# Entry of a two-block kernel: first modulation in column quarters, packed vectors on ScalarE's queue, angles ahead of the input, a late store of the input

## The reference

```
mod = silu(c) @ w_ada + b_ada            # 6 x 1024 columns: shift1, scale1, gate1, ...
u   = rmsnorm(x, g_mix) * (1 + scale1) + shift1
proj = u @ w_in                          # q, k, v, us (256 columns), two gates
y_ssm = s5(us; a_re, a_im, log_dt, b, c) # needs exp(log_dt), cos and sin of angles a_im*dt*2^j
```

## Time and profile before

| what | us |
|---|---|
| median of three runs (2013.05 to 2013.33) | 2013.3 |
| the profiled execution, its time | 2013.66 |
| the profiled execution, its span | 2011.9 |

### The profile page before, as it was taken

One profiled execution on the slowest core, in us unless ns is written; L12 is line 12 of the kernel. 1 busy time (PEld: TensorE's weight loads), 2 busy tenths in 40 slices (PEclk: granted clock), 3 DMA queues, 4 the chain that ended last, 5 costly groups with the idle time before them and its releaser, 6 DMA issues. The chain is left out here.

```text
span 2011.9 us, 25774 instructions
## 1 busy us (share of the span) xinstructions
PE 1980.5 (98%) x10047; PEld 1641.4 (82%) x10047; DVE 1100.9 (55%) x1349; ACT 647.8 (32%) x1068; POOL 1302.6 (65%) x757
## 2 busy tenths in 40 slices
PE   7999999999999999999999999999999999999998
PEld 4788988888788877888888888888888888888888
DVE  5981366767662686656622376722564554525554
ACT  4202333233431454444300045433434433211103
POOL 2638546656364459999845546876787888858650
PEclk9999999999999999999999999999999999999999
DMA  9535555544535213243573331343324222198332
GB/s 371 152 97 166 189 162 179 158 155 140 204 130 205 84 63 105 84 147 105 208 283 140 104 134 38 109 147 105 104 85 147 105 105 105 32 375 307 123 136 84
DMA packets 191945, 295.38 MB, mean 147 GB/s; under 512 B 15480, under 2 KB 139344, under 8 KB 191824
## 3 DMA queue, kind: packets, MB, share of 16 engines
q1 hardware_dynamic: 181840, 270.66, 39.6%
q10 hardware_dynamic: 9984, 23.07, 3.0%
HBM read 213.73 MB, written 79.97 MB: 146 GB/s over the span
## 5 line engine op out<-in xcount | busy, mean ns | idle before, releaser
L990 POOL TENSOR_SCALAR w_h<-raw 128x512 fp32r<-128x512 f32 (+2 forms) x108 | 237.0, 2195 | 324.7 <-issue 158.0
L1526 PE MATMUL ps<-tb,w_h 128*128 128x512 f32 x1344 | 416.9, 391 | 2.5 <-DVE quads L2819 1.9
L1076 POOL TENSOR_TENSOR w_l<-raw,w_h 128x512 fp32r<-128x512 f32 x210 | 309.8, 1484 | 92.0 <-ACT w_h L2084 92.0
L1526 PEld LDWEIGHTS ps<-tb,w_h 128*128 128x128 f32 x1344 | 251.3, 188 | 59.0 <-issue 3.8
L1526 PE MATMUL ps<-tb,w_l 128*128 128x512 f32 x672 | 261.6, 389 | 0.0
L2084 ACT ACTIVATE w_h<-raw 128x512 fp32r<-128x512 f32 x210 | 130.8, 627 | 234.6 <-PE ps L1526 153.3
L992 POOL TENSOR_TENSOR w_l<-raw,w_h 128x512 fp32r<-128x512 f32 (+2 forms) x108 | 199.7, 1849 | 9.0
L1526 PE MATMUL ps<-act_h,w_h 128*128 128x512 f32 x504 | 196.3, 389 | 0.6 <-ACT quads L2113 0.5
L1526 PE MATMUL ps<-act_h,w_l 128*128 128x512 f32 x504 | 196.1, 389 | 0.0
L1526 PE MATMUL ps<-act_l,w_h 128*128 128x512 f32 x504 | 196.1, 389 | 0.0
L1526 PEld LDWEIGHTS ps<-tb,w_l 128*128 128x128 f32 x672 | 126.2, 188 | 26.4
(11 more groups left out here) (403 smaller groups left out, 4537.9 us busy)
## 6 DMA issues: line engine op xcount, KB each, us to landing
raw<-in_w_in SPq DMA_DIRECT2D x44, 1024.0 KB, 5.4
raw<-in_w_up SPq DMA_DIRECT2D x16, 1024.0 KB, 5.3
f_scratch<-r SPq DMA_DIRECT2D x16, 1024.0 KB, 8.3
gates_scratch<-quads SPq DMA_DIRECT2D x24, 512.0 KB, 7.7
r<-gates_scratch SPq DMA_DIRECT2D x12, 1024.0 KB, 6.2
ada_lo<-in_w_ada SPq DMA_DIRECT2D x16, 512.0 KB, 3.7
ada_hi<-in_w_ada SPq DMA_DIRECT2D x16, 512.0 KB, 4.0
gates_scratch<-gate_st ACTq DMA_DIRECT2D x32, 256.0 KB, 2.7
```

The source lines that it names most:

```text
L990: nc.gpsimd.tensor_scalar(w_h[:, k, c, :], src[:, c, :], 1.0, None, ALU.mult).then_inc(s["w_high"], 1)
L1076: nc.gpsimd.tensor_tensor(w7_l[:, SLOTS[o]], x, w7_h[:, SLOTS[o]].bitcast(F32), ALU.subtract)\
L1526: last = nc.tensor.matmul(bank_of(n, bank), w[:, SLOTS[o], c, :], x(c), start=(first and c == 0 and p == 0), stop=(c == KD // 2 - 1 and p ...
```

## The change

- `w_ada` for shift1 and scale1 is loaded and used in four quarters of 256 columns (two chunks each) in place of two halves. Parts: quarter 0 in two pieces of four row chunks, quarters 1 to 3 whole. `ada_rows`, `ada_line`, `ada_columns` and the modulation on DVE go by quarters; a quarter's columns wait until the one before has been read.
- The 16 small vectors come as two packed arrays, which the host puts together without arithmetic. The identity, c, both arrays and `log_dt` are issued by ACT's queue; SP begins with x. PE transposes the packed vectors ahead of x.
- DVE makes the columns, all angles and turns ahead of the copies of x; ACT takes exp of `log_dt` and the four magnitudes ahead of the squares, and the sines behind the root.
- The first tile of `w_in` comes as chunks 0 and 1 ahead of `w_ada`, and the rest behind quarter 1. POOL splits the two chunks alone, then the others as soon as they land, and the second tile once quarter 3 is read.
- The store of x's transpose is cut: chunks 6 and 7 ahead of the second tile of `w_in`, the others behind the small arrays of the state-space branch. Its waits move: ACT waits for the first store ahead of `us`, DVE for both ahead of `krylov`.
- `s5_matrices` and `s5_local` move into the middle of units 2 and 4.

```diff
-ADA_PARTS = ((0, 0, 4), (0, 4, 7), (0, 7, 8), (1, 0, 3), (1, 3, 8))
+ADA_PARTS = ((0, 0, 4), (0, 4, 8), (1, 0, 8), (2, 0, 8), (3, 0, 8))
 # SP
-            sp.dma_start(ident[:], ...)          # and c_row
             for t in range(0, QB, 2): sp.dma_start(x_tok[:, t:t + 2, :], ...)
-            ... 16 loads into rows, log_dt
-            ada_part_in(0)
-            first_half_of(0, s["g_row_in"])
-            for i in range(1, 4):
-                ada_part_in(i)
-            first_half_of(1, w_in_[0])
-            ada_part_in(4)
-            first(1, 0)
-            sp.wait_ge(s["h_ready"], QB)
-            sp.dma_start(h_d..., h_t[:])
+            first_chunks(0, 2, s["g_row_in"])
+            for i in range(3):
+                ada_part_in(i)
+            first_chunks(2, KD, w_in_[0])
+            for i in range(3, 5):
+                ada_part_in(i)
+            sp.wait_ge(s["h_ready"], QB)
+            sp.dma_start(h_d[KD - 2:KD]..., h_t[:, KD - 2:KD, :]).then_inc(h_top_out[0], 16)
+            first(1, 0)
             ... b_in, cc, w_glu
+            sp.dma_start(h_d[0:KD - 2]..., h_t[:, 0:KD - 2, :]).then_inc(s["h_out"], 16)
 # POOL
-            split_half(0, 0, 1, s["w_half"])
+            split_first()
             pool.wait_ge(w_in_[0], 16)
-            pool.wait_ge(s["u_ready"], 1)
+            split_half(0, 0, 1, s["w_half"], lo=2)
             split_half(0, 1, 2, s["w_split"])
-            pool.wait_ge(s["u_ready"], KD - 1)
+            pool.wait_ge(s["mod_read"], 4)
 # PE
             transpose of c
+            pe.wait_ge(s["vec_in"], 32)
+            transposes of rows
             transposes of x
             keep_busy(2)
             ada_rows(0)
-            spread of both halves of 1/rms
-            ada_rows(1)
-            ada_rows(2)
-            ada_columns(0)
+            ada_rows(1)
+            spread[0]()
+            ada_columns(0)
+            spread[1]()
             keep_busy(2)
-            within={(1, 0): rows 3, (2, 2): rows 4, (3, 0): columns 1}
+            within={(0, 2): rows 2, (1, 0): columns 1, (2, 0): rows 3, (2, 2): columns 2, (4, 0): rows 4, (4, 2): columns 3}
-            between = {1: s5_matrices, 2: s5_in, 3: s5_local, 5: s5_out, 8: glu}
+            amid = {2: s5_matrices, 4: s5_local}
+            between = {2: s5_in, 5: s5_out, 8: glu}
 # ACT
+            act.dma_start(ident), (c_row), (rows_a), (rows_b), (log_dt)
             silu of c, twice
-            squares, root, exp of log_dt, magnitudes
+            exp of log_dt, magnitudes, squares, root, wait for the angles, sines
             ada_line of part 0
-            after high part 3: ada_line of half 1, sines
+            after high parts 1, 3, 5: ada_line of quarters 1, 2, 3
 # DVE
-            x copies, columns, diagonal, angles, half 0, ..., low 3, turns, half 1
+            columns, angles, turns, x copies, diagonal, step_turn, quarter 0, scaled and low 0 and 1
+            for q in range(1, 4):
+                modulation_quarter(q)
+                for c in (2 * q, 2 * q + 1):
+                    scaled(c)
+                for c in (2 * q, 2 * q + 1):
+                    low(c)
```

More of the change, by code:

```diff
@@ L519, in _ @@
                   .then_inc(x_in[t // 2], 16)
[L520 to L527, removed]
@@ L746, in _ @@
             sp.wait_ge(s["h_out"], 16)
+            sp.wait_ge(*beyond(h_top_out, 16))
             sp.wait_ge(s["gemm"], units_before(N_OUT))
@@ L1151, in product_pair @@
                     if split is not None and c == 0:
+                        pe.wait_ge(*beyond(w_first, 2))
+                    if split is not None and c == 2:
                         pe.wait_ge(s["w_half"], split + 1)
@@ L1200, in qkv_unit @@
                 for th in range(2):
+                    if th and amid is not None:
+                        amid()
                     pe.wait_ge(s["qkv_read"], AHEAD + (2 * j + th - 1 if j else 0))
@@ L1591, in spatial @@
                 pe.wait_ge(s["vn_ready"], 1)
-                pe.wait_ge(s["wst_masked"], 1)
+                pe.wait_ge(*beyond(wst_masked, 1))
                 extra_free(n)
@@ L1838, in _, with ada_row_out @@
                 step(A.activation(mag[:, :, i], par[:, 2, :], ACT.Exp, scale=float(2**i)))
-            def ada_row_out(sem, count):
-                act.wait_ge(sem, count)
-                A.activation(ada_line[:], ps[:, 2, 0:HALF], ACT.Copy).then_inc(s["c_ready"], 1)
-            ada_row_out(s["colt"], 3)
+            for t in range(QB):
+                act.wait_ge(x_in[t // 2], 16)
+                step(A.activation(sq[:, t % 2, :], x_tok[:, t, :], ACT.Square, accum_out=stat[:, 2, t:t + 1]))
+            A.activation(stat[:, 0, :], stat[:, 2, :], ACT.Sqrt, scale=1.0 / D, bias=eps_rms[:]).then_inc(s["std_ready"], 1)
+            act.wait_ge(s["s5_dve"], S5_DVE["angle_ready"])
+            step(A.activation(turn[:, 0], prep[:, 3, :, :], ACT.Sin))
+            A.activation(turn[:, 1], prep[:, 2, :, :], ACT.Sin).then_inc(s["s5_act"], 1)
+            def ada_row_out(q):
+                act.wait_ge(*((s["tr"], QB + q) if q else (s["colt"], 3)))
+                A.activation(ada_line[:], ps[:, 2, 0:NB], ACT.Copy).then_inc(s["c_ready"], 1)
+            ada_row_out(0)
             def root(sums, th, src, row=0):
@@ L3257 @@
     arrays, aps = {}, {}
-    for name, value in {**inputs, **constants()}.items():
+    packed = {name: np.concatenate([np.asarray(inputs[n], np.float32).reshape(-1) for n in rows]).reshape(-1, P)
+              for name, rows in (("rows_a", ROWS_A), ("rows_b", ROWS_B))}
+    single = {n: v for n, v in inputs.items() if n == "c" or n not in {**ROWS_A, **ROWS_B}}
+    for name, value in {**single, **packed, **constants()}.items():
         value = np.ascontiguousarray(value)
```

205 lines of the change are left out of this document (98 added, 107 removed).

## The result

The changed kernel takes 2018.4 us (median of 20 runs, 2015.45 to 2021.45), the kernel before 2014.5 in as many runs beside it (2011.26 to 2016.96; the three runs shown earlier lie in its lower third). The ratio is 1.0021, 95% interval 1.0015 to 1.0027: 4.2 us more, where I had forecast 3.8 less. The profiled execution of after has a span of 2018.0 (before: 2011.9).

A forecast was written before the change was run, and what follows sets the result against it. PE, busy 98%, was taken as the bound, so entry gains last: 3.65 - 0.6 - 0.8 + 1.55 = 3.8 us off 2013.66, minus 0.36 to the median, gives 2009.5; own range 2008 to 2011.5, full range 2004.8 to 2014.8.

The forecast's parts named there:

- L: Entry: landing time of `log_dt`, fifth load on ACT's queue, beside x; taken as 8.0 us, at the least 4.3.
- L + 21.7: Entry: exponentials, angles, x copies and PE work from `log_dt`'s landing to the first scaling (head); 29.7 against 33.36 us.
- the second tile's wait: Unit 0: PE's 1.6 us wait for POOL's second half of the second tile goes, a gain of 1.55 us.
- Splitting the first tile finds idle time: First tile of `w_in`: its split fits into idle time ahead of chunk 2, counted as 0.
- 2.5 us, which don't change: From head to first product: DVE, ACT and DVE in turn take 2.5 us, the same as before.
- The subtraction that I expected on low part 6: First product: at most one POOL subtraction, 2.4 us, holds DVE's low part 6; taken as 0.8 us of loss.
- signs of being wrong: Exponentials after 11.8, quarter rows over 3 us, low part 6 or 7 held over 2, PE waiting for `krylov` or `w_ada`.
- "slower" rival: Entry: small vectors land behind x, `log_dt` at 14.5 to 16, 2.7 to 4.2 us lost, 2016 to 2017.5; chance 0.12.
- the entry's gain or loss arrives at the end unchanged: Whole kernel: everything behind the entry is a chain of PE work, so the entry's 3.8 us gain reaches the end.
- Not handed on: Rival, state-space branch: it is the next bound, and POOL eats the cover of `krylov`; 2013 us, chance 0.08.
- the late half unit: Units 2 and 4: moving `s5_matrices` and `s5_local` half a unit later is PE order only, counted as 0.
- Vectors early: Rival, entry: small loads slip in before x fills the engines, `log_dt` at 4.3 to 5.5; about 2006.3, chance 0.18.

The follow-up runs named there:

- e4: The kernel before with only the matrix step moved into the middle of unit 2 and the local step into unit 4; 2013.6 us, ratio 0.9997.
- e2: The changed kernel with its five small loads issued first on SyncE's queue, ahead of x, instead of on ScalarE's; 2009.0 us, ratio 0.9976.
- e8: The changed kernel with `log_dt` first instead of last of the five small loads on ScalarE's queue; 2017.4 us, ratio 1.0016.
- e10: The changed kernel with the transposes of the input's fourth tile done six times instead of once, to fill TensorE's idle time; 2017.1 us, ratio 1.0022.
- e16: The kernel of e10 unaltered, run again for a second profile; no separate time given, unit 0 at 77.67 us instead of 72.66.
- e6: The changed kernel with small loads first on SyncE's queue, plus 67 products of 16 columns ahead of the input's transposes; 2032.8 us against 2009.0 without them.

## Why the prediction was wrong

**The step that failed is L.** I took 8.0 for the landing of `log_dt`; it is 12.6 in all three profiles. Both terms were short: the fifth issue stands at 3.09 and not 2.4, because ScalarE's issues take up to 0.73, and the way takes 9.5 where I had 5.7. The packets of the trace show which part of the 5.7 was wrong. Queue 1 carries x, queue 10 the small loads; the three stretches of the profile after are 7 to 9, 4.5 to 6.5 and 9.5 to 12.2 us (packets, MB, share of 16 engines).

```profile
q1 hardware_dynamic: 197, 0.74, 90.6%
q10 hardware_dynamic: 196, 0.08, 14.8%
```

```profile
q1 hardware_dynamic: 208, 0.79, 98.3%
q10 hardware_dynamic: 32, 0.01, 1.9%
```

```profile
q1 hardware_dynamic: 159, 0.62, 75.3%
q10 hardware_dynamic: 106, 0.01, 2.1%
```

From 7 to 9 the two queues take turns packet by packet, as I had counted: equal numbers, and the starts of the small packets lie most often 174 to 180 ns apart, which is one packet of x (159) and a small one. But for 2 us x runs nearly alone, and the pieces of `log_dt` then take 2.7 us, during which x is slow as well. I had counted neither; their cause is open.

By the Trainium skill, DMA: Bandwidth & Descriptors, section Queues, rings and completion order, an engine stays with one queue for a whole packet of 9 to 17 descriptors, from which I had an estimate of 10 to 16 for L. The measured 12.6 lies in it, and my 8.0 had set the rule aside. But the turns from 7 to 9 are of one packet each, which is not that rule; whether the 2 us of x alone are such a turn no run here shows.

**The chain behind L came out in its sum, in part by luck.** L + 21.7 gives 34.3; measured 34.81. The rows of a quarter take 1.87 (forecast 2.16), the product 30.57 (31.75), the second tile's wait is gone (1.6). With L = 12.6 my own sum gives a loss of 0.8; the entry lost 0.9 in the first profile, but 0.4 and 2.6 in the other two. Single terms were off and cancelled. "Splitting the first tile finds idle time" and "2.5 us, which don't change" were wrong: beside GpSimd's split of that tile the low part of the first half chunk took 1.81 instead of 0.75 in the first profile, so the first product begins 3.56 us after the head. The product was shorter than forecast by 1.2. The subtraction that I expected on low part 6 came a little later (4.62 us for low parts 6 and 7 instead of 2.48), and it is low part 7 that was held: 3.42 us instead of 1.28, one of my signs of being wrong; TensorE waited 0.31 for it. Another of these signs decided: the exponentials came at 12.60, after 11.8.

So the "slower" rival had the mechanism, small loads held back by x, and the point 11.8 right, at a chance of 0.12 that was too low; its L of 14.5 to 16 was too late. Against it I held that the other queue had moved mixed packets; that was no reason.

**The second step that failed** is that the entry's gain or loss arrives at the end unchanged. The lag of 0.9 grew to 6.1 in the first profile, 0.4 to 1.2 in the second, 2.6 to 5.1 in the third. The wait at the gate tile is in all three (0.46 to 1.54 us), and no rival had it: the change moves TensorE's instruction packets. Of the rest, 1.6 us behind the matrix step in two of the three profiles, and nothing in the other, goes with the stretches at 1.2 GHz, which differ from execution to execution. Why the changed kernel has more of them than the kernel before is not shown, and their share of the 4.2 us between the runs stays open.

**"Not handed on" and the late half unit:** TensorE never waits for `krylov`, and e4 gives the moved steps a price of zero within its interval, as forecast. **Vectors early** describes the entry of e2: at L = 5.4 the head is 26.18 (L + 20.8), 8.6 us earlier than after. Its time, 2006.3, was not reached (2009.0): side by side with the profile of before, e2 is 7.4 us ahead at unit 0, 5.8 behind the matrix step, where its stretch is 6.83 us, 4.9 behind the gate tile, which is late there too, and 4.7 at the end.

## What to carry to other kernels

A small load that something waits for belongs ahead of the bulk on the bulk's own queue; on a second queue beside it, it took 4.2 to 9.5 us here instead of 1.7 to 2.9, and reordering the second queue only passed the delay on (e8). Before work is moved ahead of a queue of copies, ask what its last input is and when that lands. And a kernel bound by TensorE can lose a microsecond hundreds of microseconds behind an edit, so lay the two traces side by side to the end before the loss is put down to the place of the edit.

## What the runs showed of the hardware

Three executions of one program had 6.83, 3.41 and 6.83 us at 1.2 GHz at the same place, and one, one and two stretches in the entry; another (e10, e16) had none and two. A single profile does not give the price of such a stretch, and the mean granted clock counts them even where TensorE is idle. A packet of 16 KB of instructions held one transfer engine for 0.95 us, and a load of 1 MB that it fell into was started on 1.3 to 2.4 us later than in the kernel before. Packets of two queues took turns one by one from 7 to 9 us. An f32 product of 16 columns with 128 x 128 weights took 0.43 us (e6).
